# Attention units in another order, rotary embedding on VectorE, and a longer first landing ring in a two-layer float32 kernel

## The reference, cut to what matters

```python
mod = silu(c) @ w_ada + b_ada                       # 6 x 2048 numbers
shift_m, scale_m, gate_m, shift_f, scale_f, gate_f = split(mod, 6)
h = rmsnorm(x) * (1 + scale_m) + shift_m
dq, dk, dv, q_lat, kv_lat, k_pe = split(h @ w_in)   # 1024, 1024, 1024, 512, 256, 64 columns
dq, dk = partial_rope(dq, 16), partial_rope(dk, 16) # of each 64, the first 16
o_diff = rmsnorm((softmax(q0 k0) - lam * softmax(q1 k1)) @ dv)   # 8 heads, two maps each
q  = rmsnorm(q_lat)  @ w_q_b                        # 8 heads of 128 + 64 (rotated)
kv = rmsnorm(kv_lat) @ w_kv_b                       # 8 heads of 128 keys + 128 values
o_mla = softmax([q_nope q_rope] [k_nope k_rope]) @ v             # 8 heads, one map each
x = x + gate_m * (concat(o_diff, o_mla) @ w_out)
x = x + gate_f * (relu(h2 @ w_ff1)**2 @ w_ff2)      # h2: normed and modulated with shift_f, scale_f
```

## Time and profile before

| | us |
|---|---|
| median of 3 runs | 2202.97 (2202.71 to 2207.62) |
| profiled execution: its own time | 2207.75 |
| profiled execution: span from first to last instruction | 2206.0 |
| TensorE busy with matmuls | 2012.2 (91%) |
| VectorE busy | 1306.4 (59%) |
| ScalarE busy | 944.5 (43%) |
| GpSimd busy | 231.9 (11%) |
| moved by DMA | 448.83 MB, mean 203 GB/s |

### The profile page before, as it was taken

One profiled execution on the slowest core, in us unless ns is written; L12 is line 12 of the kernel. 1 busy time (PEld: TensorE's weight loads), 2 busy tenths in 40 slices (PEclk: granted clock), 3 DMA queues, 4 the chain that ended last, 5 costly groups with the idle time before them and its releaser, 6 DMA issues. The chain is left out here.

```text
span 2206.0 us, 24619 instructions
## 1 busy us (share of the span) xinstructions
PE 2012.2 (91%) x9240; PEld 1643.0 (74%) x9240; DVE 1306.4 (59%) x2002; ACT 944.5 (43%) x1428; POOL 231.9 (11%) x243
## 2 busy tenths in 40 slices
PE   6787778768799999999999999989989999999999
PEld 2276666556678888888888878878978877787877
DVE  3787877786794555555555555566565545545544
ACT  2354343453454344434434454454444444444432
POOL 0100353100100110010010022110111001101000
PEclk9899989878999999999999999989999999999999
DMA  8798878648795555556565555534535356656644
GB/s 311 291 339 301 304 260 288 211 142 289 278 319 183 191 189 183 184 189 190 182 191 185 187 193 161 174 99 123 165 115 149 123 177 195 189 181 184 191 171 162
DMA packets 128968, 448.83 MB, mean 203 GB/s; under 512 B 14288, under 2 KB 14544, under 8 KB 128336
## 3 DMA queue, kind: packets, MB, share of 16 engines
q1 hardware_dynamic: 124928, 433.74, 59.8%
q0 software_dynamic: 1568, 7.34, 0.9%
q10 hardware_dynamic: 2352, 6.17, 0.7%
HBM read 443.00 MB, written 4.19 MB: 203 GB/s over the span
## 5 line engine op out<-in xcount | busy, mean ns | idle before, releaser
L282 DVE TENSOR_TENSOR wlo<-raw,whi 128x1024 fp32r<-128x1024 f32 (+4 forms) x652 | 785.5, 1208 | 765.3 <-ACT whi L281 721.8
L281 ACT ACTIVATE whi<-raw 128x1024 fp32r<-128x1024 f32 (+4 forms) x652 | 658.1, 1011 | 874.7 <-PE g L387 736.4
L382 PE MATMUL g<-whi,lhsA_hi 128*128 128x512 f32 (+4 forms) x1840 | 713.0, 389 | 37.1 <-DVE lhsA_lo L774 27.0
L383 PE MATMUL g<-whi,lhsA_lo 128*128 128x512 f32 (+4 forms) x1840 | 695.1, 379 | 0.0
L387 PE MATMUL g<-wlo,lhsA_hi 128*128 128x512 f32 (+4 forms) x1840 | 466.0, 375 | 0.2 <-DVE wlo L282 0.2
L382 PEld LDWEIGHTS g<-whi,lhsA_hi 128*128 128x128 f32 x1840 | 355.3, 193 | 98.7 <-ACT tmp L766 23.0
L383 PEld LDWEIGHTS g<-whi,lhsA_lo 128*128 128x128 f32 x1840 | 355.5, 193 | 54.3 <-issue 1.7
L387 PEld LDWEIGHTS g<-wlo,lhsA_hi 128*128 128x128 f32 x1840 | 340.8, 191 | 55.8 <-DVE wlo L282 0.4
L526 DVE SCALAR_TENSOR_TENSOR raw<-raw,srow 128x1024 f32<-128x1024 f32 x192 | 234.3, 1242 | 40.7 <-DMA raw<-in_w_ada 40.2
L382 PE MATMUL g<-whi,lhsF_hi 128*128 128x512 f32 x512 | 203.4, 397 | 0.0
L383 PE MATMUL g<-whi,lhsF_lo 128*128 128x512 f32 x512 | 201.9, 394 | 0.0
(11 more groups left out here) (286 smaller groups left out, 1565.8 us busy)
## 6 DMA issues: line engine op xcount, KB each, us to landing
raw<-in_w_ff SPq DMA_DIRECT2D x256, 512.0 KB, 3.5
raw<-in_w_ada SPq DMA_DIRECT2D x192, 512.0 KB, 5.0
raw<-in_w_in SPq DMA_DIRECT2D x176, 512.0 KB, 4.1
raw<-in_w_out SPq DMA_DIRECT2D x64, 512.0 KB, 5.1
raw<-in_w_in SPq DMA_DIRECT2D x80, 384.0 KB, 3.1
raw<-in_w_mem_kv SPq DMA_DIRECT2D x16, 512.0 KB, 5.8
raw<-in_w_branch_a SPq DMA_DIRECT2D x12, 512.0 KB, 3.7
...
```

What stands on the lines that cost most here:

```text
L281: t_hi = AC.put(lambda e: e.activation(hi, x, ACT.Copy), landed, free, us=0.2 + n * 0.00167)
L282: t_lo = DV.put(lambda e: e.tensor_tensor(lo, x, hi.bitcast(F32), ALU.subtract), landed, t_hi, free, us=0.15 + n * 0.00208)
L382: PE.put(lambda e, o=o, x=xh, w=h, f=first: e.matmul(o, x, w, start=f, stop=False), w, mark=False, us=us)
L383: PE.put(lambda e, o=o, x=xl, w=h: e.matmul(o, x, w, start=False, stop=False), mark=False, us=us)
```

## The change

- `order1` is h2 h3 l0 h0 l1 **h4 l2 l3 h1 h5** (before: h2 h3 l0 h0 l1 h1 l2 h4 l3 h5).
- `w_out` is rotated by 1024 rows, so pairs 0 to 3 of the left operand take the latent heads and pairs 4 to 7 the difference heads. As the half units read pairs 4 to 7 alone, pairs 0 to 3 are emptied right after l3, and `mla_end` starts there. Of the first two output units the first four tiles each run before the rest of the first; nothing is lent any more.
- `rope` runs on VectorE, six instructions for both halves of the rows. The copies of `g_q` are one ScalarE instruction; the latent key and value unit is evacuated by four ScalarE instructions that put keys and values where they belong, without GpSimd.
- Up to the end of the memory units the landing ring has nine buffers (four more, `raw_wide`, in memory that is freed afterwards; `narrow`), and native tiles are fetched up to three ahead.
- `spread` waits for the newest TensorE instruction in place of the newest GpSimd one, as `rot` was written by VectorE.
- `half_unit` pumps with a width of 4 (before 2), and the output units with 2 steps for each tile.
- The small vectors `vec` are allocated with 240 in place of 208 columns, which moves what is allocated behind them by 128 bytes in each partition.

```diff
@@ -17,7 +17,7 @@
 LAM0 = 0.8 - 0.6 * float(np.exp(-0.0))
-NRAW, NSPLIT = 5, 4
+NRAW, NSPLIT, NWIDE = 5, 4, 4
@@ -159,7 +159,7 @@
     cst = sb("cst", [P, C_END])
-    vec = sb("vec", [P, 208])[:, 0:V_END]
+    vec = sb("vec", [P, 240])[:, 0:V_END]
@@ -252,15 +252,16 @@
-    raw_sem = [[sem(f"s_raw{i}"), 0] for i in range(NRAW)]
-    raw_free = [[] for _ in range(NRAW)]
-    state = dict(slot=0, split=0, nsplit=0, unit=0)
+    slots = [raw[:, i, :] for i in range(NRAW)]
+    raw_sem = [[sem(f"s_raw{i}"), 0] for i in range(NRAW + NWIDE)]
+    raw_free = [[] for _ in raw_sem]
+    state = dict(slot=0, ring=NRAW + NWIDE, split=0, nsplit=0, unit=0)
 ...
     def fetch(src, n):
-        i = state["slot"] % NRAW
+        i = state["slot"] % state["ring"]
         state["slot"] += 1
-        x, free = raw[:, i, 0:2 * n], raw_free[i]
+        x, free = slots[i][:, 0:2 * n], raw_free[i]
@@ -284,6 +285,10 @@
+    def narrow():
+        state["ring"], state["slot"] = NRAW, 0
@@ -338,18 +343,23 @@
-    def run(u, steps=1, width=2, adas_per_pair=0):
-        par = state["unit"] % 2
-        state["unit"] += 1
+    def run(u, steps=1, width=2, adas_per_pair=0, lo_i=0, hi_i=None):
+        if lo_i == 0:
+            u["par"] = state["unit"] % 2
+            state["unit"] += 1
+        par = u["par"]
 ...
             b.free = []
-        for i, j in enumerate(u["tiles"]):
-            consume_to(j + (2 if plan[j][2] else 4))
+        for i, j in list(enumerate(u["tiles"]))[lo_i:hi_i]:
+            ahead = j + (3 if plan[j][2] else 4)
+            while plan[j][2] and not plan[min(ahead, len(plan)) - 1][2]:
+                ahead -= 1
+            consume_to(ahead)
@@ -388,7 +398,7 @@
             pump(steps, width)
-        u["tok"], u["par"] = tok, par
+        u["tok"] = tok
@@ -453,15 +463,13 @@
-    def mix(us, row=0, native=False, later=0):
+    def mix(us, row=0, native=False):
 ...
             u = dict(n=n, K=K, lhs=lhs, tiles=[], k_off=k_off, pairs=list(range(K // 2)))
-            if len(built) < later:
-                u["pairs"] = u["pairs"][K // 4:] + u["pairs"][:K // 4]
-            for k0 in [2 * p for p in u["pairs"]]:
+            for k0 in range(0, K, 2):
@@ -476,13 +484,16 @@
-    order1 = (("h", 2), ("h", 3), ("l", 0), ("h", 0), ("l", 1), ("h", 1), ("l", 2), ("h", 4), ("l", 3), ("h", 5))
+    order1 = (("h", 2), ("h", 3), ("l", 0), ("h", 0), ("l", 1), ("h", 4), ("l", 2), ("l", 3), ("h", 1), ("h", 5))
 ...
             u_q.extend(mix([("w_q_b", 384 * i, 384, 4, lhs_q), ("w_kv_b", 512 * i, 512, 2, lhs_kv)]))
-    u_out = mix([("w_out", 512 * i, 512, 16, A_) for i in range(4)], later=1)
+    u_out = mix([("w_out", 512 * i, 512, (0, 8), A_) for i in range(2)])
+    for u, v in zip(u_out, mix([("w_out", 512 * i, 512, (8, 8), A_) for i in range(2)])):
+        u["tiles"], u["pairs"] = u["tiles"] + v["tiles"], list(range(8))
+    u_out += mix([("w_out", 512 * i, 512, 16, A_) for i in range(2, 4)])
@@ -560,7 +571,7 @@
-        used_ = [PO.tok()]
+        used_ = [PE.tok()]
@@ -614,6 +625,8 @@
     lhs_mem.hi = sb("lhsM", [P, 16, 256], F32, start)
+    wide_raw = sb("raw_wide", [P, NWIDE, 1024], F32, start)
+    slots += [wide_raw[:, i, :] for i in range(NWIDE)]
@@ -746,6 +759,7 @@
     t_of["mv"] = evac2(par, tok, 512, mv, t_of["rm"], scale=(rm[:, 0:1], rm[:, 1:2]))
+    narrow()
@@ -801,17 +815,14 @@
-        for t in range(2):
-            cos = trig[:, t, c0:c0 + half].rearrange("p (a w) -> p a w", a=1).to_broadcast([P, segs, half])
-            sin = trig[:, t, c0 + half:c0 + 2 * half].rearrange("p (a w) -> p a w", a=1).to_broadcast([P, segs, half])
-            r = [x[:, 0:segs * half].rearrange("p (s w) -> p s w", w=half) for x in rot]
-            u, v = x1[:, t], x2[:, t]
-            w = [tok, t_of["trig"], [PO.tok()]]
-            ks = [PO.put(lambda e, o=o, i0=i0, i1=i1: e.tensor_tensor(o, i0, i1, ALU.mult), *w)
-                  for o, i0, i1 in ((r[0], u, cos), (r[1], v, sin), (r[2], v, cos), (r[3], u, sin))]
-            PO.put(lambda e, r=r, u=u: e.tensor_tensor(u, r[0], r[1], ALU.subtract), ks)
-            k = PO.put(lambda e, r=r, v=v: e.tensor_tensor(v, r[2], r[3], ALU.add), ks)
-        return k
+        cos = trig[:, :, c0:c0 + half].rearrange("p t (a w) -> p t a w", a=1).to_broadcast([P, 2, segs, half])
+        sin = trig[:, :, c0 + half:c0 + 2 * half].rearrange("p t (a w) -> p t a w", a=1).to_broadcast([P, 2, segs, half])
+        r = [x[:, 0:2 * segs * half].rearrange("p (t s w) -> p t s w", t=2, w=half) for x in rot]
+        w = [tok, t_of["trig"], [DV.tok()]]
+        ks = [DV.put(lambda e, o=o, i0=i0, i1=i1: e.tensor_tensor(o, i0, i1, ALU.mult), *w, us=0.2)
+              for o, i0, i1 in ((r[0], x1, cos), (r[1], x2, sin), (r[2], x2, cos), (r[3], x1, sin))]
+        DV.put(lambda e: e.tensor_tensor(x1, r[0], r[1], ALU.subtract), ks, us=0.2)
+        return DV.put(lambda e: e.tensor_tensor(x2, r[2], r[3], ALU.add), ks, us=0.2)
@@ -836,7 +847,7 @@
                   r.ap[:, :, 288:320].rearrange("p t (s w) -> p t s w", s=1), 1, 32, 16, ks)
-        kr = PO.put(lambda e: e.tensor_copy(r.ap[:, :, 320:384], r.ap[:, :, 256:320]), kr)
+        kr = DV.put(lambda e: e.tensor_copy(r.ap[:, :, 320:384], r.ap[:, :, 256:320]), kr)
@@ -948,11 +959,11 @@
             yield
-            split_from(T, 2, [vec[:, V_SUB:V_SUB + 1]] * 2, lhsA, 4 * j + 2 * p, tok)
+            split_from(T, 2, [vec[:, V_SUB:V_SUB + 1]] * 2, lhsA, 8 + 4 * j + 2 * p, tok)
 ...
     def mla_head(h):
-        for name in (("qn", h // 2), ("vm", h // 2), "krT"):
+        for name in (("qn", h // 2), ("kn", h // 2), ("vm", h // 2), "krT"):
@@ -1019,7 +1030,7 @@
         yield
-        split_from(T, 2, [1.0, 1.0], lhsA, 8 + 2 * p, tok)
+        split_from(T, 2, [1.0, 1.0], lhsA, 2 * p, tok, t_of["latents"])
@@ -1043,8 +1054,8 @@
         T.release([kq])
-        kc = PO.put(lambda e: e.tensor_copy(r.ap[:, :, 384:448], r.ap[:, :, 128:192]), k)
-        kc = PO.put(lambda e: e.tensor_copy(r.ap[:, :, 448:512], r.ap[:, :, 320:384]), k)
+        kc = AC.put(lambda e: e.activation(r.ap[:, :, 384:512].rearrange("p t (s w) -> p t s w", w=64),
+                                           v[:, :, :, 128:192], ACT.Copy), k, us=0.4)
@@ -1054,34 +1065,38 @@
     def g_kv(r, ks, i):
-        for j in range(2):
-            kv_ = PO.put(lambda e, j=j: e.tensor_copy(vm[:, :, 256 * i + P * j:256 * i + P * j + P],
-                                                      r.ap[:, :, 256 * j + P:256 * j + 2 * P]), ks, fence)
         T = yield from grab(TB)
-        tok = turn_rows(T, [r.ap[:, t, 256 * j:256 * j + P] for j in range(2) for t in range(2)], ks)
+        tok = turn_rows(T, [r.ap[:, t, P * j:P * j + P] for j in range(2) for t in range(2)], ks)
 ...
         mark(("kn", i), kn)
-        mark(("vm", i), kv_)
-        r.release([tok, kv_])
+        r.release([tok])
 ...
         if i < 4:
-            got = run(u_in[i])
+            got = run(u_in[i], width=4)
 ...
             j = i - 4
-            mark(("dv", j), sum_parts(run(u_in[i]), i, dv[:, :, 512 * j:512 * j + 512], fence))
+            mark(("dv", j), sum_parts(run(u_in[i], width=4), i, dv[:, :, 512 * j:512 * j + 512], fence))
 ...
         bg.appendleft(g_q(r, ks, i))
-        r, ks = row_unit(u_q[2 * i + 1], steps=2, width=4)
+        par, tok = run(u_q[2 * i + 1], steps=2, width=4)
+        r = take(rows)
+        got = [G[2 * par + t].rearrange("p (s w) -> p s w", w=256) for t in range(2)]
+        ks = [AC.put(lambda e, t=t: e.activation(r.ap[:, t, 0:256].rearrange("p (s w) -> p s w", w=P), got[t][:, :, 0:P],
+                                                 ACT.Copy), tok, r.free, us=0.4) for t in range(2)]
+        kv = [AC.put(lambda e, t=t: e.activation(vm[:, t, 256 * i:256 * i + 256].rearrange("p (s w) -> p s w", w=P),
+                                                 got[t][:, :, P:2 * P], ACT.Copy), tok, fence, us=0.4) for t in range(2)]
+        gfree[par] = ks + kv
+        mark(("vm", i), kv)
@@ -1111,10 +1126,13 @@
             latent_units(i)
-    lhsA.ready = [None] * 8
+            if i == 3:
+                lhsA.ready[0:4] = [None] * 4
+                t_of["latents"] = [PE.tok()]
+                for p in range(4):
+                    bg.append(mla_end(p))
+    lhsA.ready[4:8] = [None] * 4
     bg.append(spread(0, gate_free))
-    for p in range(4):
-        bg.append(mla_end(p))
@@ -1132,11 +1150,9 @@
     bg.append(reload())
-    lend()
-    while any(t is None for t in lhsA.ready[4:]):
-        pump(1, 6)
-    give_back()
-    first_out = run(u_out[0], width=6)
+    for u in u_out[0:2]:
+        run(u, steps=2, width=4, hi_i=4)
+    first_out = run(u_out[0], steps=2, width=6, lo_i=4)
@@ -1173,7 +1189,7 @@
     for j in range(4):
-        add_in(run(u_out[j]) if j else first_out, j, gt, True, lambda j=j: gate(0, j))
+        add_in(run(u_out[j], lo_i=4 * (j == 1)) if j else first_out, j, gt, True, lambda j=j: gate(0, j))
@@ -1693,6 +1709,7 @@
```

(1 more changed line is left out.)

## The result

The changed kernel takes 2190.37 us (median of 6 runs, 2185.78 to 2195.18) against 2202.9 for the kernel before on the same chip: ratio 0.9936, 95% interval 0.9918 to 0.9954. By the medians that is 12.5 us faster (14 by the ratio) where 49.5 were forecast, and 0.4 us outside the range. The profiled execution has a span of 2188.6 us (before 2206.0, so 17.4 less; that execution of the kernel before stands 4.8 us above its median).

What follows compares the result with a forecast made beforehand. It blamed TensorE's 72.7 us idle and 30.9 us of half clock between 236.8 and 594.1 us. Idle -31.2, clock -13.3, forced products +2, landing -7 gave -49.5: 2154 us, own range 2136 to 2172, overall 2115 to 2190.

Steps and rivals of the forecast that it cites:

- GpSimd's waits: Mixed units and heads, 236.8 to 422.4 us: of 24.2 us of transposes waiting for GpSimd, 19.2 go.
- Order of the units: Heads alone, 422.4 to 484.6 us: eight output tiles beside heads 4 to 7 cut TensorE's idle 22.8 us to 9.
- heads in C: Mixed units and heads, 236.8 to 422.4 us: four heads moved in bring 7.5 us more idle, bounds 0 and 15.
- The clock: From 236.8 to 594.1 us: time lost to TensorE's half clock scales with idle time, 30.9 us to 17.6.
- The residual's load: Output units, to 594.1 us: load leaves some 5 us earlier, so TensorE's idle falls from 10.7 us to 5.
- Landing buffers: Memory stretch, 17.6 to 104.9 us: 10 of 14.2 us of weight waits won, 3 lost to memory rows, 7 net.
- Products late: Ahead of the feed-forward part: 12 fewer modulation products done, one or two forced there, costing 2 us (bounds 0 and 6).
- Padding: Tiles behind the small vectors move by 128 bytes: costed at 0, 2 us either way.
- Bytes set the pace: Rival, 0.06: 236.8 to 594.1 us cannot exceed its mean 253 GB/s; only the landing stage wins, 2196 to 2203 us.
- The heads set the pace: Rival, 0.20: heads 4 to 7 on two score banks take as long as eight did; idle and clock stay, 2176 us.
- VectorE becomes the bound: Rival, 0.08: 15.1 us more VectorE work at the same busy share makes 236.8 to 594.1 us 20 longer, 2216 us.
- The signs: New profile if right: GpSimd's busy time down some 75 us, clock near 0.95, first feed-forward unit near 560 us.

Runs made afterwards that it cites:

- p_pool: The kernel before with only the rotation and its copies taken off GpSimd, old order and landing ring: 2188.78 us, ratio 0.9935.
- b_fill: Kernel before plus rotation off GpSimd, nine landing buffers and late ScalarE squares, planner's lead for modulation products 6 us, not 3: 2201.21 us, ratio 0.9980.
- f_new: The changed kernel with 84 of the 192 modulation products left out: 2155.98 us, ratio 0.9779 to the kernel before.
- f_old: c_pool_ring (old order of units) with the same 84 of 192 modulation products left out: 2156.93 us, ratio 0.9780 to the kernel before.
- c_pool_ring: The kernel before with rotation off GpSimd and the nine-buffer landing ring, in the old order of units: 2183.62 us, ratio 0.9909.
- a_old_list: The changed kernel with the old `order1` list, two output units still begun beside the last heads: 2186.98 us, ratio 0.9907 to the kernel before.
- p_ring: The kernel before with only the nine landing buffers and native tiles fetched one further ahead: 2199.85 us, ratio 0.9987.
- a_late_sq: The changed kernel with ScalarE's squares of each output unit put behind the next unit's splits: 2181.53 us, ratio 0.9893 to the kernel before.

## Why the prediction was wrong

The direction was right, and so was the size of the largest single term; the term of the new order failed in sign, and the padding, costed at nothing, was worth a third of what the parts without the order gave. By spans the whole -17.4 splits into -18.6 (p_pool), -4.8 (ring on top, 2187.4 to 2182.6), -8.3 (padding, by the rows of `lhsF_hi`; not run alone) and, as what is left, +14.3 for the new order. By the ratios the parts are -14.3 and -5.7, and +14.2 is left.

- **GpSimd's waits, -19.2.** In p_pool C is 22.8 us shorter, and TensorE's idle time in it fell from 39.2 to 18.1; 7.3 come back behind the start of the feed-forward part, as 150 products are done by then and not 172. The rotation took 0.29 us an instruction on VectorE, about what I took from the earlier trace rows. But the reason was only half right, and the size in part luck: the planner, whose estimates changed with the part, also put 35 products into C where 58 had been. At b_fill's 1.07 us each those 23 are worth as much as the whole gain of C. How much the waits alone were worth, at 58 products, was not run.
- **Order of the units: D's idle 22.8 to 9, heads in C +7.5.** This is the step that failed: -6.3 said for the idle time, about -9 with its share of the clock, and +14.3 measured as the balance (+7 to +8 without the late products: f_new and f_old are equal, with 8.3 of padding in f_new's favour). I had laid 21.8 us of tiles into 22.8 us of gaps *by work*. But TensorE's idle time did not fall: up to the eighth output tile it is 27.4 us, 25.0 in c_pool_ring, and with the old list the begun tiles raise it to 34.1 (a_old_list). The gaps are waits for a head's steps on other engines, and neither tiles nor products stood in them for nothing: 27 products fewer in D make it 17.6 us shorter (f_new).
- **What the order's parts cost.** Four heads did not leave D for C: D has the last products of eight heads before and after, as two difference heads moved out and two latent ones in; C has the scores of eleven heads where it had eight. The list made C 16.1 us longer and D+E 10.1 shorter; by the ratios it costs 6 us (changed against a_old_list), and beginning the output units in place of lending the banks, with what goes with that, costs 8 (a_old_list against c_pool_ring, the padding's 8.3 taken off), each with an interval of some 5 us. The loss of the lent banks, which I named and priced within a bound, is not shown by itself.
- **The clock, -13.3.** It followed idle time as said, but the idle time stayed: C to E have 64.7 us of it (72.7 before, 41.5 said) and clocks of 0.92, 0.83 and 0.94, not near 0.95. By the prediction's own estimate 26.8 us went to the clock (30.9 before, 17.6 said).
- **The residual's load, -5.** Nothing. The load was asked for at 516.9 us, 0.2 behind the end of the first output unit's matmuls instead of 2.3, where I had said 5 us earlier; GpSimd then stood 9.9 us for it instead of 8.2, and TensorE's stall is 7.6 us instead of 7.0. The stall is real, though, and worth 9 us when ScalarE's squares no longer stand ahead of the splits.
- **Landing buffers, -7.** The 14.2 us went, and the memory rows were hardly delayed: the first matmul on them starts at 17.69 us (17.60 before), the first on a weight tile at 20.78 (20.22), and their median time to landing went from 16.2 to 17.5. That is 0.1 to 1.3 us where I had set 3. The estimate of about 3.5 us, worked out from the Trainium skill, *DMA: Bandwidth & Descriptors* (Queues, rings and completion order), was too high as well. But a 13-us wait for the keys came in place of the 14.2, which I had not looked for: -3.2 (p_ring, by the medians), and -4.8 on top of the rotation part.
- **Products late, +2.** About right: without the padding's 8.3 us the rest is 4 us longer than before. The 12 products fewer at the end of E came as forecast (158), but by luck: I let their number follow time, of which C to E lost only 6.8 us. It follows the planner.
- **Padding, 0.** -8.3. No row before could tell it.
- **The rivals.** "Bytes set the pace" (2196 to 2203) came nearest in number, by chance: the output units run at 349 GB/s in a_late_sq, well above 253. "The heads set the pace" (2176) named most of the mechanism: D kept its idle time. It left out what the list costs in C and the products in D. "VectorE becomes the bound" (2216) fell by its condition, as VectorE is busy for 0.81 of C in b_fill; but from 35 to 69 products in C each one does cost nearly its length, and the planner kept off that.
- **The signs.** GpSimd's busy time fell by 74 us (231.9 to 157.9) and its waits in C went, as said. The feed-forward part starts at 596.6 us and not near 560.
